# Multiply before the first half of the down weights: a reordering on VectorE in an expert loop

## The chip, the cores and the metric

The kernel runs on one core of one Trainium2 chip. The metric is device time in microseconds (us) for one launch that computes both request groups through both layers. Each engine of the core (TensorE or PE, VectorE or DVE, ScalarE or ACT, GpSimd or POOL, SyncE or SP) has its own instruction stream, runs it in order, and meets the others only through semaphores.

## The reference, cut to what matters

Two layers of an encoder work on 2 x 256 tokens of width 1024. In each layer an attention part is followed by a mixture of experts, and the change is in the latter:

```
for e in range(16):
    a   = silu(t @ w_gate[e]) * (t @ w_up[e])        # 512 wide
    out = out + gate[:, e:e+1] * (a @ w_down[e])     # 1024 wide
```

`gate` is zero but for two experts of each token. The inputs and weights are float32.

## The kernel before, in words

**Tiles.** After the router, VectorE works out a plan: the chosen (token, expert) pairs are sorted by expert into tiles of 128 rows with one expert each. In the run shown here there are 16 tiles in each layer, 14 in a loop over pairs of tiles and two behind it (`last=True`). A tile is even (`par` 0) or odd (`par` 1); each parity has its own ring slots for weights and its own half of the row buffers.

**Two-part arithmetic.** A product of float32 matrices is made of three products of a faster format. ScalarE copies a weight half (128x2048) into a high part (`high`, line 1293) and VectorE subtracts that from the original to get the low part (`low`, line 1865). TensorE then runs low x high, high x low and high x high into one bank (lines 947 to 949 for gate and up, 962 to 964 for down). A tile has six such halves, or parts: up 0 and 1, gate 0 and 1, down 0 and 1; each is 12 matmuls. The high parts go round four buffers, so part number `at + i` waits until part `at + i - 4` has been used (`part_used`).

**Order on TensorE in tile n:** transposes of the gathered rows of tile n+1 (line 927, waits for the gather); up 0 and up 1 of n; gate 0 of n+1; transposes of the activated rows of n (line 935, waits for `a_ready`); gate 1 of n+1; down 0 and down 1 of n (wait for `aT_lo_ready` and the low parts). In what follows a tile's start is the start of its line 927.

**Order on ScalarE in tile n:** high part of the rows of n+1 (line 1300); SiLU of the gate result of n (line 1314); `high` of gate 1 of n+1 (at+3), of down 0 (at+4) and of down 1 (at+5); `aT_hi`, the high part of the transposed activation (line 1321); `high` of up 0, up 1 and gate 0 of the tiles that follow (at+6, at+7, at+8); the two copies of the result to `y_row` (line 1330).

**Order on VectorE in tile n:** low part of the rows of n+1 (line 1874); `low` at+3; `low` at+4; the multiplication of SiLU and up (line 1891), which waits until up 1 is done (`part_used`) and for `silu_ready`, and raises `a_ready`; `low` at+5; `aT_lo` (line 1894), which waits for `aT_hi`; `low` at+6, at+7, at+8. The `low` instructions read two tiles of SBUF; lines 1874, 1891 and 1894 read one bank of PSUM and one tile of SBUF.

**Order on GpSimd in tile n:** copy the row indices for tile n+2 (`row_now`, line 1975), drain, gather its rows from HBM (line 1957); wait for the result of tile n (`y_ready`), copy its indices (line 1975), drain, scatter its rows to HBM (line 1962); wait until they have landed. As this is one stream, the gather of tile n+3 is issued only after the scatter of tile n has landed. The gather issued while TensorE is in tile n+1 is the one whose rows are transposed at the start of tile n+2.

**SyncE** loads 2 MB of weights for each of gate, up and down of each tile, each as soon as the part that frees its slot has been used (line 631).

Of the kernel before, what the change touches and what calls it, by code (L numbers as in the profile page):

```python
# [303 lines left out]
def build_trunk(nc, t_in, y_prompt, y_sample):  # L304
# [7 lines left out]
    with ctx:  # L312
# [1049 lines left out]
        def _(dve):  # L1362
# [25 lines left out]
            at = PAR["b_ada"]  # L1388
# [10 lines left out]
            at = PAR["neg_lam"]  # L1399
# [116 lines left out]
            with dve.Fori(0, DEPTH) as layer:  # L1516
# [344 lines left out]
                def low(k, par, h, buf, at):  # L1861

                    dve.wait_ge(part_hi_ready, at + 1)
                    cols = slice(h * 2048, (h + 1) * 2048)
                    v.tensor_tensor(w_low[EXPERT_SLOTS[par][k]][:, cols], ring[EXPERT_SLOTS[par][k]][:, cols],  # L1865
                                    part_hi[buf].bitcast(F32), ALU.subtract)\
                        .then_inc(part_lo_ready, 1)

                def rows_low(n, par):

                    dve.wait_ge(xg_hi_ready, n + 1)
                    for half in range(2):
                        at = (slice(None), par, slice(4 * half, 4 * half + 4), slice(None))
                        ins = v.tensor_tensor(xg_lo[at].rearrange("p c n -> p (c n)"), bank[4 + half][:, :],
                                              xg_hi[at].rearrange("p c n -> p (c n)").bitcast(F32), ALU.subtract)
                    ins.then_inc(xg_lo_ready, 1)

                def expert(p, par, last=False):
                    n = (before + p) * 2 + par
                    ends_here = last and par == 1  # L1880
                    first = 2 + 6 * par
                    at = (before + p) * 12 + first
                    buf = [(first + i) % 4 for i in range(9)]
                    if not ends_here:
                        rows_low(n + 1, 1 - par)
                        low(0, 1 - par, 1, buf[3], at + 3)
                    d = 2 if ends_here else 4
                    low(2, par, 0, buf[d], at + d)
                    dve.wait_ge(part_used, PARTS_BEFORE + at + 2)
                    dve.wait_ge(silu_ready, n + 2)  # L1890
                    v.tensor_tensor(act_rows, bank[1][:, :], silu[:, par, :], ALU.mult).then_inc(a_ready, 1)
                    low(2, par, 1, buf[d + 1], at + d + 1)
                    dve.wait_ge(aT_hi_ready, n + 1)
                    v.tensor_tensor(aT_lo.rearrange("p f n -> p (f n)"), bank[6][:, :],
                                    aT_hi.rearrange("p f n -> p (f n)").bitcast(F32), ALU.subtract)\
                        .then_inc(aT_lo_ready, 1)
                    if not ends_here:
                        for h in range(2):
                            low(1, 1 - par, h, buf[6 + h], at + 6 + h)
                    if not last:  # L1900
                        low(0, par, 0, buf[8], at + 8)
# [7 lines left out]
                with dve.Fori(0, rest) as p:  # L1909
                    for par in range(2):  # L1910
                        expert(p, par)
                for par in range(2):
                    expert(rest, par, last=True)
# [111 lines left out]
```

## Time and profile before

| | us |
|---|---|
| Median of 3 runs (1803.8 to 1806.64) | 1805.65 |
| The profiled execution's own time | 1801.19 |
| Its span, first to last instruction | 1799.3 |
| PE busy (matmul) | 1523.4 (85%) |
| DVE busy | 1052.2 (58%) |
| ACT busy | 886.8 (49%) |
| POOL busy | 136.5 (8%) |

The two expert loops take about 540 to 884 us and 1411 to 1755 us of the span. Busy time is a share over the whole span; what is late in a stretch is read from the waits and from the order of time. A row of the time line gives start and duration in us, engine, line, operation, tiles, shapes and count, and in brackets the idle time of the engine before it and what ended it. Rows that follow each other closely may be merged (x2), and their first number is then the start of the first. The duration of a DMA row on POOL is that of issuing it, not of the transfer.

### The profile page before, as it was taken

To read this page: it belongs to the slowest core of one execution; us is meant where nothing else is said; L and a number is where in the kernel's file an instruction comes from. 1 tells how busy PE (TensorE), PEld (TensorE's weight loads), DVE (VectorE), ACT (ScalarE), POOL (GpSimd) and SP (SyncE) were. 2 spreads that over 40 slices of the span, in tenths; PEclk is the share of its full clock that TensorE was granted. 3 is DMA by queue.
4 is the path that set the end of the run, shared out by engine and by line. 5 is a ranking of instruction groups with operands and counts; after the bars stand their busy time and mean duration, and the time that the engine had idled before them with its cause. 6 is when DMAs were issued, how large, how long until landed. Compare 5 with 4: busy or idle time off the path is not lost.

```text
span 1799.3 us, 19037 instructions
## 1 busy us (share of the span) xinstructions
PE 1523.4 (85%) x6494; PEld 1081.9 (60%) x6494; DVE 1052.2 (58%) x1339; ACT 886.8 (49%) x1146; POOL 136.5 (8%) x141
## 2 busy tenths in 40 slices
PE   3799987999957999999469989799997489999984
PEld 1477545666725777777327765466664477777762
DVE  2645469222466788778253825942244688778755
ACT  2532348111236777786244224731133477777743
POOL 2000000000001121211000000000000112121200
PEclk9899997999977999999789989799998699999997
DMA  8622570111237999998392147202113789999923
GB/s 244 226 94 94 188 234 1 47 47 52 89 141 275 346 346 339 334 336 298 131 326 94 47 141 257 71 22 72 47 50 137 254 307 348 322 336 338 324 100 143
DMA packets 164692, 341.82 MB, mean 190 GB/s; under 512 B 26214, under 2 KB 28912, under 8 KB 164496
## 3 DMA queue, kind: packets, MB, share of 16 engines
q1 hardware_dynamic: 150752, 314.58, 50.0%
q0 software_dynamic: 10800, 23.09, 3.4%
q10 hardware_dynamic: 3072, 3.28, 0.7%
q8 instruction: 38, 0.62, 0.1%
q14 instruction: 30, 0.25, 0.0%
HBM read 333.58 MB, written 24.12 MB: 199 GB/s over the span
## 4 chain that ended last, share of the span: by engine, by line
PE 58%; DVE 11%; ACT 9%; issue 9%; DMA 8%; SPq 3%; ACTq 1%; POOLq 1%; DVEq 0%
PE bank L684 9%; PE bank L685 8%; PE bank L686 8%; PE bank L879 6%; DMA y_by_choice<-zone,row_now 3%; DMA zone<-rows_by_token,row_now 3%; PE bank L962 3%; PE bank L964 3%; PE bank L963 3%; PE bank L715 2%; SPq L582 2%; PE bank L832 2%; PE bank L947 2%; PE bank L949 2%; PE bank L948 2%
## 5 line engine op out<-in xcount | busy, mean ns | idle before, releaser
L684 PE MATMUL bank<-x_hi,w_lo 128*128 128x512 f32 x608 | 257.3, 423 | 20.0 <-DVE x_lo L1451 8.4
L686 PE MATMUL bank<-x_hi,w_hi 128*128 128x512 f32 x608 | 238.2, 392 | 0.0
L685 PE MATMUL bank<-x_lo,w_hi 128*128 128x512 f32 x608 | 238.2, 392 | 0.0
L1865 DVE TENSOR_TENSOR w_lo<-ring,zone_r 128x2048 fp32r<-128x2048 f32 x92 | 210.4, 2290 | 27.6 <-ACT zone_r L1293 27.6
L1293 ACT CAST x_lo<-ring 128x2048 fp32r<-128x2048 f32 x96 | 183.6, 1914 | 66.5 <-PE bank L949 30.7
L1293 ACT CAST zone_r<-ring 128x2048 fp32r<-128x2048 f32 x96 | 181.6, 1910 | 20.4 <-PE bank L964 13.9
L947 PE MATMUL bank<-w_lo,zone_r 128*128 128x512 f32 x384 | 160.2, 417 | 5.8 <-issue 5.8
L684 PEld LDWEIGHTS bank<-x_hi,w_lo 128*128 128x128 f32 x608 | 114.9, 189 | 62.2 <-issue 30.0
L1428 DVE TENSOR_TENSOR w_lo<-ring,w_hi 128x1024 fp32r<-128x1024 f32 x84 | 102.0, 1221 | 85.1 <-ACT w_hi L1088 84.6
L685 PEld LDWEIGHTS bank<-x_lo,w_hi 128*128 128x128 f32 x608 | 115.2, 190 | 31.3 <-issue 9.6
L686 PEld LDWEIGHTS bank<-x_hi,w_hi 128*128 128x128 f32 x608 | 115.0, 189 | 24.6
L1251 ACT ACTIVATE zone<-bank 128x512 f32<-128x512 f32 x32 | 19.1, 597 | 216.7 <-PE bank L686 216.7
L1865 DVE TENSOR_TENSOR w_lo<-ring,x_lo 128x2048 fp32r<-128x2048 f32 x36 | 82.3, 2292 | 61.4 <-ACT x_lo L1293 61.4
L879 PE MATMUL bank<-zone,ring 128*128 128x512 f32 x256 | 115.8, 595 | 0.9
L948 PE MATMUL bank<-x_lo,zone_r 128*128 128x512 f32 x272 | 111.0, 408 | 0.0
L949 PE MATMUL bank<-x_lo,zone_r 128*128 128x512 f32 x272 | 110.9, 408 | 0.0
L1088 ACT CAST w_hi<-ring 128x1024 fp32r<-128x1024 f32 x84 | 87.1, 1044 | 22.9 <-DMA ring<-in_w_in 6.1
L949 PE MATMUL bank<-zone_r 128*128 128x512 f32 x240 | 94.9, 395 | 0.0
L948 PE MATMUL bank<-zone_r 128*128 128x512 f32 x240 | 94.4, 393 | 0.0
L947 PEld LDWEIGHTS bank<-w_lo,zone_r 128*128 128x128 f32 x384 | 75.3, 196 | 21.9 <-issue 6.6
L715 PE MATMUL bank<-ring,cs 128*32 128x512 f32 x384 | 53.8, 684 | 36.1 <-DMA ring<-in_w_ada 35.6
L1954 POOL DMA_DIRECT2D rows_by_token<-zone x8 | 4.4, 548 | 999.2 <-ACT zone L1280 998.4
(255 smaller groups left out, 2743.6 us busy)
## 6 DMA issues: line engine op xcount, KB each, us to landing
ring<-in_w_gate SPq DMA_DIRECT2D x32, 2048.0 KB, 13.7
ring<-in_w_up SPq DMA_DIRECT2D x32, 2048.0 KB, 14.7
ring<-in_w_down SPq DMA_DIRECT2D x32, 2048.0 KB, 9.2
ring<-in_w_ada SPq DMA_DIRECT2D x24, 2048.0 KB, 8.8
ring<-in_w_in SPq DMA_DIRECT2D x14, 2048.0 KB, 7.9
ring<-in_w_out SPq DMA_DIRECT2D x4, 2048.0 KB, 7.7
zone<-y_by_choice SPq DMA_DIRECT2D x8, 1024.0 KB, 8.1
ring<-in_w_in SPq DMA_DIRECT2D x16, 256.0 KB, 7.1
```

The lines of the kernel that those rows point to most:

```text
L684: mm(out, lo, x_first, start=start, stop=False)
L685: mm(out, hi, x_second, start=False, stop=False)
L686: return mm(out, hi, x_first, start=False, stop=stop)
L715: ins = mm(ps[32 * j:32 * (j + 1), :], cs[:, k, :], w[:, k, :], start=(k < 4), stop=(k >= KC - 4))
L879: ins = mm(ps[:, :], w[:, k, j * P:(j + 1) * P], oT[:, k, :], start=(k == 0), stop=(k == 3))
L947: mm(out, xg_hi[:, par, c, :], wv[:, c, :], start=(c == 0), stop=False)
L948: mm(out, xg_lo[:, par, c, :], hi[:, k, :], start=False, stop=False)
L949: ins = mm(out, xg_hi[:, par, c, :], hi[:, k, :], start=False, stop=(c == KC - 1))
L1088: nc.scalar.copy(w_hi[:, n % W_BUFS, :, :], group_view(ring[SLOT[b]], b, c)).then_inc(S["w_hi_ready"], 1)
L1293: nc.scalar.copy(part_hi[buf], ring[EXPERT_SLOTS[par][k]][:, h * 2048:(h + 1) * 2048])\
L1428: v.tensor_tensor(group_view(w_lo[SLOT[b]], b, c), group_view(ring[SLOT[b]], b, c), w_hi[:, n % W_BUFS, :, :].bitcast(F32), ALU.subtract). ...
L1865: v.tensor_tensor(w_low[EXPERT_SLOTS[par][k]][:, cols], ring[EXPERT_SLOTS[par][k]][:, cols], part_hi[buf].bitcast(F32), ALU.subtract)\
```

## The change

One line of VectorE's part of the expert loop moves down, behind the multiplication. Its waits go with it (they are inside `low`).

```diff
                         low(0, 1 - par, 1, buf[3], at + 3)
                     d = 2 if ends_here else 4
-                    low(2, par, 0, buf[d], at + d)
                     dve.wait_ge(part_used, PARTS_BEFORE + at + 2)
                     dve.wait_ge(silu_ready, n + 2)
                     v.tensor_tensor(act_rows, bank[1][:, :], silu[:, par, :], ALU.mult).then_inc(a_ready, 1)
+                    low(2, par, 0, buf[d], at + d)
                     low(2, par, 1, buf[d + 1], at + d + 1)
```

The helper that it calls:

```
                def low(k, par, h, buf, at):
                    dve.wait_ge(part_hi_ready, at + 1)
                    cols = slice(h * 2048, (h + 1) * 2048)
                    v.tensor_tensor(w_low[EXPERT_SLOTS[par][k]][:, cols], ring[EXPERT_SLOTS[par][k]][:, cols],
                                    part_hi[buf].bitcast(F32), ALU.subtract)\
                        .then_inc(part_lo_ready, 1)
```

`part_lo_ready` counts in the same order as before: the order of the `low` instructions among themselves does not change. No instruction is added or removed.

## Rows read from the trace of the kernel before

**Rows 1.** The page, its fourth part: the chain that ended last, by line.

```profile
PE bank L684 9%; PE bank L685 8%; PE bank L686 8%; PE bank L879 6%; DMA y_by_choice<-zone,row_now 3%; DMA zone<-rows_by_token,row_now 3%; PE bank L962 3%; PE bank L964 3%; PE bank L963 3%; PE bank L715 2%; SPq L582 2%; PE bank L832 2%; PE bank L947 2%; PE bank L949 2%; PE bank L948 2%
```

**Rows 2.** PE's waits: us, times, longest; L935 twice: first, then second layer's loop.

```profile
PE bank L935 <- DVE root L1891: 14.3, 15, 2.4
...
PE bank L935 <- DVE root L1891: 16.3, 16, 2.5
...
PE bank L927 <- DMA zone<-rows_by_token,row_now: 7.5, 8, 1.4
```

**Rows 3.** Busy time by stretch, two pairs of tiles; the last three: clock, DMA share, GB/s.

```profile
1511.44:1551.53 40.09, 36.87 (x169) 29.20 (x169) 32.12 (x21) 31.31 (x27) 8.27 (x8) 1.00 0.97 348
...
1591.64:1633.12 41.48, 38.24 (x169) 30.51 (x169) 32.08 (x21) 31.13 (x26) 8.09 (x8) 0.96 0.92 330
```

**Rows 4.** Time line of PE in the pair 1511.44 to 1551.53.

```profile
1511.44 1.09 PE L927 MATMUL bank<-const,zone 128*128 128x128 f32 x8 [1.10 <-DMA zone<-rows_by_token,row_now]
...
1522.72 0.66 PE L935 MATMUL bank<-const,root 128*128 128x128 f32 x4 [1.87 <-DVE root L1891]
...
1526.02 0.39 PE L962 MATMUL bank<-w_lo,zone_r 128*128 128x512 f32 x1
...
1531.72 1.09 PE L927 MATMUL bank<-const,zone 128*128 128x128 f32 x8
...
1541.40 0.66 PE L935 MATMUL bank<-const,root 128*128 128x128 f32 x4 [0.21 <-DVE root L1891]
...
1551.53 1.09 PE L927 MATMUL bank<-const,zone 128*128 128x128 f32 x8 [1.09 <-DMA zone<-rows_by_token,row_now]
```

**Rows 5.** Time line of DVE in the same pair, around the multiplications.

```profile
1517.57 2.29 DVE L1865 TENSOR_TENSOR w_lo<-ring,x_lo 128x2048 fp32r<-128x2048 f32 x1 [2.41 <-ACT x_lo L1293]
1519.78 2.29 DVE L1865 TENSOR_TENSOR w_lo<-ring,zone_r 128x2048 fp32r<-128x2048 f32 x1
1521.98 0.68 DVE L1891 TENSOR_TENSOR root<-bank,tmp 128x512 f32<-128x512 f32 x1
1522.58 2.28 DVE L1865 TENSOR_TENSOR w_lo<-ring,zone_r 128x2048 fp32r<-128x2048 f32 x1
1524.78 0.69 DVE L1894 TENSOR_TENSOR zone_r<-bank,zone_r 128x512 fp32r<-128x512 f32 x1
...
1538.46 2.28 DVE L1865 TENSOR_TENSOR x_hi<-ring,x_lo 128x2048 fp32r<-128x2048 f32 x1
1540.66 0.68 DVE L1891 TENSOR_TENSOR root<-bank,tmp 128x512 f32<-128x512 f32 x1
1541.26 2.28 DVE L1865 TENSOR_TENSOR x_hi<-ring,x_lo 128x2048 fp32r<-128x2048 f32 x1
1543.46 0.68 DVE L1894 TENSOR_TENSOR zone_r<-bank,zone_r 128x512 fp32r<-128x512 f32 x1
1544.51 4.59 DVE L1865 TENSOR_TENSOR w_lo<-ring,zone_r 128x2048 fp32r<-128x2048 f32 x2 [0.37 <-ACT zone_r L1293]
```

**Rows 6.** Time line of POOL in the same pair.

```profile
1512.82 1.02 POOL L1962 DMA_INDIRECT y_by_choice<-zone,row_now  x1 [0.94 <-issue]
1521.39 0.71 POOL L1975 COPY row_now<-row_i 128x1 int32 x1 [7.55 <-DMA y_by_choice<-zone,row_now]
1523.05 2.71 POOL L1957 DMA_INDIRECT zone<-rows_by_token,row_now  x1 [0.94 <-issue]
...
1542.35 1.23 POOL L1975 COPY row_now<-row_i 128x1 int32 x1 [6.98 <-DMA y_by_choice<-zone,row_now]
1544.49 1.02 POOL L1957 DMA_INDIRECT zone<-rows_by_token,row_now  x1 [0.91 <-issue]
```

**Rows 7.** Line L1957 in the second layer: durations (min/median/max) and its transfers.

```profile
L1957 POOL DMA_INDIRECT zone<-rows_by_token,row_now x14: 1012/1028/2725, 1423.2 to 1707.8; - x14
...
DMA to landing us min/median/max: 6.4/7.4/8.8
```

**Rows 8.** Time line of ACT in the odd tile of that pair.

```profile
1542.09 0.59 ACT L1321 CAST zone_r<-bank 128x512 fp32r<-128x512 f32 x1 [1.73 <-PE bank L935]
1542.57 1.91 ACT L1293 CAST zone_r<-ring 128x2048 fp32r<-128x2048 f32 x1
```

## The prediction

> **What bounds the kernel now.** I read the chain that ended last, then PE's waits in the loops, then one pair of tiles instruction by instruction. The chain [rows 1] holds two entries that are no engine's work: the scatter of results and the gather of rows, 3% each, some 54 us each of 1799. So in the loops there is a path through GpSimd and the DMA besides the one through PE. PE's waits [rows 2] say the same: it waits for the multiplication (L1891) 14.3 + 16.3 = 30.6 us in the two loops, about once in each tile, and for the gather in every second tile. The first wait is what the edit aims at; the second may take its place.
>
> The pair 1511.44 to 1551.53 is a plain one: granted clock 1.00 (the 2.4 GHz level), 40.09 us, DMA engines 97% busy at 348 GB/s [rows 3]. Its even tile takes 1531.72 - 1511.44 = 20.28 us and its odd tile 19.81 us [rows 4]. In the even tile PE waits 1.87 us for the multiplication, in the odd one 0.21 us. The next even tile starts only when its gather has landed (1.09 us of idle time, 1.10 in front of this one). The odd tile starts with none shown, but 1531.72 is also 5.96 us after its own gather was issued (1523.05 + 2.71 = 1525.76 [rows 6]), and the other gather took 6.02 us from the end of its issue (1544.49 + 1.02 = 1545.51) to PE's start at 1551.53. So both starts hang on gathers, the odd one just so.
>
> Now how GpSimd and VectorE meet. The gather in the odd tile is issued in 1.02 us, the one in the even tile in 2.71 us; 1.03 is the median of the 14 and 2.73 the maximum [rows 7]. The long one started at 1523.05 inside a `low` (1522.58 to 1524.86 [rows 5]) and ended 0.90 us after it. The small index copies do the same: that of 1542.35 ended at 1543.58, 0.04 after the `low` that ran until 1543.54; that of 1521.39 ended at 1522.10, 0.03 after the `low` that ran until 1522.07, though the multiplication had by then begun. I read this as: a GpSimd instruction that begins while a `low` (two SBUF inputs) runs waits for its end, and the multiplication and `aT_lo` (one PSUM input) let it through. The gather at 1544.49 was spared narrowly: the next `low` began at 1544.51, 0.02 us behind it, and only because VectorE had been idle for 0.37 us for ScalarE.
>
> The **Trainium skill** (SBUF — State Buffer, section "Who interferes with whom") says that a DVE instruction with two SBUF inputs contends with a GpSimd instruction that reads SBUF, and the later one blocks fully until the first has finished; by the rows above the trace agrees for the copies. The same section infers that a tensor_tensor does not stall descriptor generation, as that needs only the write side. By that inference the gathers would never be held by a `low` and the time would be that of the rival "no change" below; the 2.71 us speak against it, so I don't follow it.
>
> **The change, part by part.** The multiplication waits for up 1 and SiLU, both done before `low` at+3 ends in either tile, so it moves ahead by one `low`, 2.20 us (1521.98 - 1519.78).
>
> Even tile. The multiplication runs 1519.78 to 1520.46; PE had nothing else to do from 1522.72 - 1.87 = 1520.85 on, so that wait is gone. What is late next is `aT_lo`: the three instructions `low` at+4, multiplication, `low` at+5 take the same time in any order, so it still ends at 1525.47. Down 0 starts then instead of at 1526.02 [rows 4]: the gain is about 0.5 us out of 1.87. The odd tile could start 0.5 us earlier, but its gather has to be there.
>
> Odd tile. In the same way 0.2 to 0.4 us of PE are saved (its wait, 0.21 as shown; up to 0.38 when the overlap of matmuls is counted). ScalarE's `aT_hi` (1542.09) and the `high` of at+6 behind it (1542.57 to 1544.48 [rows 8]) come earlier by as much: that `high` ends at 1544.1 to 1544.3. And here the cover goes: `low` at+6 no longer waits for ScalarE. It starts right behind `aT_lo`, at 1544.1 to 1544.3 instead of 1544.51. The gather does not move: its index copy was held until the end of `low` at+5 (1543.54, unchanged), and the drain of 0.91 puts it at 1544.49. Now it is 0.2 to 0.4 us behind the start of a `low` instead of 0.02 in front. It waits for the end of `low` at+6 (1544.13 + 2.29 = 1546.42) and ends 0.90 later, at 1547.32 instead of 1545.51: 1.81 us late. With 6.02 us to landing the next even tile starts at 1553.34: the odd tile takes 21.62 instead of 19.81 us.
>
> Back in the even tile, the scatter of the odd tile before it was sent in time while the tile started 1.8 + 0.4 us later, so it lands 2.2 us earlier against the tile's start: 1521.39 becomes about tile + 7.7 instead of tile + 9.95. The index copy is then held by `low` at+3 (until tile + 8.4) and slips through at the multiplication. The gather starts at tile + 9.3, is held by `low` at+4 (until tile + 11.2) and ends at about tile + 12.1 instead of tile + 14.32; it lands at tile + 18.1 and PE finishes the tile at tile + 19.6, which now sets the odd start. Even tile 19.6 instead of 20.28.
>
> The new pair: 19.6 + 21.6 = 41.2 us, 1.1 us more. Of the 16 tiles of a layer, counted from 0, the odd ones 1 to 13 each issue a gather on which the start of the next even tile (2 to 14) hangs: seven in each layer, 14 x 1.1 = 15.5 us. Off go about 0.9 us in each layer for the last two tiles, which have no gather behind them (-1.8), and about 1.5 us for the pairs in which the clock fell to 0.96 and PE took 41.48 us [rows 3], part of which is now hidden behind the gather. Sum: +12 us.
>
> **Unknown sizes, from both sides.** (1) DMA from gather issue to landing: from the shortest (6.4 - 1.02 = 5.4 us) to the longest (8.8 - 2.72 = 6.1) [rows 7]. The delayed gather meets a little less weight traffic. At 5.4 the odd tile is 21.0 us, the pair 40.6, the sum +4. Below that the scatter lands in the even tile's `low` at+4 as now and the even tile goes back to 20.3, so a held gather can hardly gain. I take 6.0, which both of this pair's gathers show. (2) Whether GpSimd gets in between two `low` instructions with no gap. No row of before shows a GpSimd instruction begun in the first of two such. If it does, the wait is as above. If VectorE keeps what they share, the gather waits for at+7 too, 2.2 us more: odd tile 23.8, pair 43.4, 14 x 3.3 - 1.8 = +45 us. I take the first: at the border between a `low` and a multiplication GpSimd was let in 0.03 us after the `low` ended. (3) VectorE itself being held by GpSimd: the `low` behind the gather at 1544.49 began and lasted as the others, so nothing.
>
> **Rivals.**
> A, the forecast: the odd gather is caught by `low` at+6 and released behind it. +12 us, range +3 to +20.
> B: caught and held over two `low` instructions, +45 us. For it: the two are adjacent, with the second ready; against it: point (2).
> C, no change: the odd gather gets through (a lead of 0.2 to 0.4 us is shorter than the 0.47 at which 1523.05 was caught, and the skill's inference of above would also let it through), or its transfer catches up. Then both starts still hang on gathers that do not move: even tile 20.28, odd 19.81, and only the last tiles gain. -2 to +3 us.
> D, the other side, faster: PE's order decides and the gathers follow. It is decided by the landing: if gathers take less than about 5.5 us, or index copies fall into a multiplication's gap and not into a `low`, PE gains its 0.5 + 0.4 us in each of the 16 pairs (8 in each layer): at most 14 us, as `aT_lo` is next. For it: tiles with PE at once behind the gather's landing exist, the even start waits only 1.1 us. Against it: the gather chain is in the chain of the end [rows 1] and nothing of the edit shortens it. A naive reader would take the whole 30.6 us; `aT_lo` excludes that. -5 to -14 us.
>
> **Numbers.** A 0.54, B 0.18, C 0.13, D 0.15. The sum was made against the profiled execution: 1801.19 + 12 = 1813.2 (its span 1799.3, with 1.9 around it). The runs' median lies 4.5 above that execution, and I add the 12 to the median: 1805.65 + 12 = 1817.6, rounded to 1817.5. A alone: 1809 to 1826. The range reaches from just under the median, cutting most of D, up to B's 1805.65 + 46: 1801 to 1852. A measurement of this kernel can tell about 0.2% (3.6 us) from no change: faster is D, 0.15; the same is C and A's edge, 0.14; slower 0.71.
>
> **What would show it.** PE's wait for L1891 falls from 30.6 us to near nothing, and a wait for `aT_lo` (L1894) appears before L962, 1.0 to 1.5 us in even tiles. POOL's L1957 in odd tiles lasts about 2.8 us instead of 1.02 (B: about 5), and ends 0.9 behind the end of a `low`. PE's wait in front of even tiles for the gather grows from 1.1 to about 3.3 us; pairs take about 41.2 us. I am wrong if L1957 in odd tiles stays at 1.02 us, or if it is longer and the even tiles still start 19.8 us after the odd ones; and my reading of the stall falls if instructions held on POOL don't end with a `low`.

## The result, and the profile after

| | before | changed |
|---|---|---|
| Median of 4 runs | 1804.72 us | 1823.44 us |
| Lowest to highest | 1798.8 to 1806.64 | 1814.78 to 1828.55 |
| Profiled execution | 1801.19 us | 1814.78 us |

The ratio on record is 1.0089, 95% interval 1.0059 to 1.0118: 16 us slower, 11 to 21 by the interval (the two medians alone lie 18.7 apart). 1817.5 had been forecast (+12), slower with a chance of 0.71.

The chain that ended last (the page, its fourth part) now has more of the gathers and scatters, 7% and 6% where there were 3% each [rows 1]:

```profile
PE bank L684 8%; PE bank L686 8%; PE bank L685 8%; DMA zone<-rows_by_token,row_now 7%; DMA y_by_choice<-zone,row_now 6%; PE bank L879 6%; DVE w_lo L1865 2%; PE bank L962 2%; PE bank L715 2%; SPq L582 2%; PE bank L832 2%; PE bank L964 2%; PE bank L963 2%; PE bank L947 2%; PE bank L949 2%
```

PE's waits in the two loops (total us, times, longest), first layer, then second. They answer to [rows 2]. The multiplication is now line 1890.

```profile
PE bank L927 <- DMA zone<-rows_by_token,row_now: 21.1, 7, 4.0
...
PE bank L962 <- DVE w_lo L1865: 9.2, 7, 1.4
...
PE bank L935 <- DVE root L1890: 0.9, 1, 0.9
...
PE bank L927 <- DMA zone<-rows_by_token,row_now: 21.2, 7, 3.3
...
PE bank L962 <- DVE w_lo L1865: 5.0, 4, 1.4
```

The wait for the multiplication is gone (30.6 us before, one of 0.9 left). In its place stand 7 waits of some 3 us in each layer for the gather, and, in most even tiles, one of 1.4 in front of down 0. The last are labelled with `low` (L1865); VectorE's order below shows that the `aT_lo` behind it (line 1894, 1573.39 to 1574.07) is what ends just before down 0 starts at 1574.27.

One pair of tiles, PE, then DVE, then POOL (start, duration, engine, line), to be laid beside [rows 4 to 6]:

```profile
1560.23 1.09 PE L927 MATMUL bank<-const,zone 128*128 128x128 f32 x8 [3.16 <-DMA zone<-rows_by_token,row_now]
...
1574.27 0.50 PE L962 MATMUL bank<-w_lo,zone_r 128*128 128x512 f32 x1 [1.39 <-DVE w_lo L1865]
1579.88 1.03 PE L927 MATMUL bank<-const,zone 128*128 128x128 f32 x8
...
1601.55 1.09 PE L927 MATMUL bank<-const,zone 128*128 128x128 f32 x8 [3.15 <-DMA zone<-rows_by_token,row_now]
```

```profile
1568.99 4.48 DVE L1865 TENSOR_TENSOR w_lo<-ring,zone_r 128x2048 fp32r<-128x2048 f32 x2
1573.39 0.68 DVE L1894 TENSOR_TENSOR zone_r<-bank,zone_r 128x512 fp32r<-128x512 f32 x1
...
1586.66 0.68 DVE L1890 TENSOR_TENSOR root<-bank,tmp 128x512 f32<-128x512 f32 x1
1587.27 4.48 DVE L1865 TENSOR_TENSOR x_hi<-ring,x_lo 128x2048 fp32r<-128x2048 f32 x2
1591.67 0.68 DVE L1894 TENSOR_TENSOR zone_r<-bank,zone_r 128x512 fp32r<-128x512 f32 x1
1592.27 4.51 DVE L1865 TENSOR_TENSOR w_lo<-ring,zone_r 128x2048 fp32r<-128x2048 f32 x2
```

```profile
1561.06 1.03 POOL L1962 DMA_INDIRECT y_by_choice<-zone,row_now  x1 [2.45 <-issue]
1569.25 2.07 POOL L1975 COPY row_now<-row_i 128x1 int32 x1 [7.17 <-DMA y_by_choice<-zone,row_now]
1572.24 2.12 POOL L1957 DMA_INDIRECT zone<-rows_by_token,row_now  x1 [0.93 <-issue]
...
1590.76 1.03 POOL L1975 COPY row_now<-row_i 128x1 int32 x1 [7.03 <-DMA y_by_choice<-zone,row_now]
1592.70 2.74 POOL L1957 DMA_INDIRECT zone<-rows_by_token,row_now  x1 [0.91 <-issue]
```

In the odd tile `low` at+6 begins at 1592.27 and the gather at 1592.70, 0.43 us behind it. The gather takes 2.74 us instead of 1.02 and ends at 1595.44, 0.9 us behind the first of the two `low` instructions (1592.27 + 2.29 = 1594.56), not behind the second. All 14 gathers of odd tiles took 2.74 to 2.76 us. The odd tile takes 21.67 us, the even one 19.65: 41.3 us for the pair.

Where the whole time went, by stretch (length, then busy time of PE, PEld, DVE, ACT, POOL; granted clock, DMA share, GB/s). Each kernel: tiles 0 to 14 of layer 1, its last pair up to the last scatter, what lies between the loops, and the two loop stretches of layer 2. First the kernel before:

```profile
561.25:844.09 282.84, 260.41 (x1178) 206.72 (x1176) 226.00 (x141) 218.10 (x182) 53.93 (x52) 0.99 0.91 327
844.09:882.91 38.82, 31.97 (x136) 25.08 (x136) 19.93 (x14) 18.23 (x18) 3.53 (x6) 0.96 0.20 72
882.91:1431.53 548.62, 455.18 (x1890) 301.12 (x1891) 264.22 (x488) 197.57 (x362) 6.57 (x9) 0.90 0.38 131
1431.53:1714.83 283.30, 260.49 (x1177) 206.88 (x1175) 225.87 (x141) 217.90 (x182) 53.00 (x52) 0.99 0.92 328
1714.83:1753.69 38.86, 31.99 (x136) 25.09 (x136) 19.96 (x14) 18.26 (x18) 3.55 (x6) 0.95 0.18 63
```

and the changed one:

```profile
561.26:850.31 289.05, 258.52 (x1177) 206.00 (x1175) 224.01 (x141) 217.58 (x182) 63.99 (x53) 0.99 0.90 321
850.31:892.26 41.95, 33.15 (x136) 25.97 (x136) 19.37 (x13) 18.21 (x17) 3.36 (x5) 0.92 0.14 56
892.26:1434.88 542.62, 451.02 (x1891) 300.62 (x1892) 264.31 (x488) 197.74 (x362) 6.74 (x9) 0.91 0.39 132
1434.88:1724.72 289.84, 263.08 (x1177) 209.50 (x1176) 224.36 (x141) 217.73 (x182) 64.78 (x53) 0.98 0.90 322
1724.72:1767.22 42.50, 33.70 (x136) 26.42 (x136) 19.53 (x13) 18.32 (x17) 3.38 (x5) 0.88 0.12 49
```

The loops up to tile 14 are 6.2 + 6.5 = 12.8 us longer, the last pairs 3.1 + 3.6 = 6.8 us. Together 19.5 us, of which the stretch between the loops, where nothing was changed, gives 6.0 us back in this execution (548.62 to 542.62). So the loops lose more than the 13.6 us between the two profiled executions, and the 16 us of the ratio lie between the two figures.

The last pair's loss, which I had not forecast, has a place. In the last tile PE goes from its transposes straight to down 0 (PE, layer 1; before, then changed):

```profile
869.19 0.66 PE L935 MATMUL bank<-const,root 128*128 128x128 f32 x4 [0.87 <-DVE root L1891]
872.13 0.49 PE L962 MATMUL bank<-x_hi,zone_r 128*128 128x512 f32 x1 [2.28 <-DVE x_hi L1865]
```

```profile
875.16 0.66 PE L935 MATMUL bank<-const,root 128*128 128x128 f32 x4 [0.87 <-DVE root L1890]
880.30 0.79 PE L962 MATMUL bank<-x_hi,zone_r 128*128 128x512 f32 x1 [4.49 <-DVE x_hi L1865]
```

From the transposes to down 0 it is 5.14 us instead of 2.94. There the `low` of down 0 used to run while VectorE waited for up 1. Behind the multiplication it is in the open, and no part of gate 1 lies in between to hide it. The first matmul of layer 1 also shows the lower clock level (0.79 us against 0.49; in layer 2 it is 0.79 against 0.69). PE's busy time in the last pairs grows by 1.2 and 1.7 us at the same 136 matmuls, which is the rest of the 3.1 and 3.6 us.

### The profile page after: what moved, and what is told of

Same layout as the page of the kernel before. It is cut to its first block, busy times and chain, and to the rows that moved or that the text cites. A ratio compares the mean times of both kernels' runs of the same rounds, so it can differ in the third digit from the quotient of the medians.

```text
span 1812.8 us, 19037 instructions
## 1 busy us (share of the span) xinstructions
PE 1524.7 (84%) x6494; PEld 1087.5 (60%) x6494; DVE 1047.8 (58%) x1339; ACT 886.4 (49%) x1146; POOL 158.0 (9%) x141
## 4 chain that ended last, share of the span: by engine, by line
PE 55%; DMA 15%; DVE 11%; issue 8%; ACT 7%; SPq 3%; POOLq 1%; ACTq 1%; DVEq 0%
PE bank L684 8%; PE bank L686 8%; PE bank L685 8%; DMA zone<-rows_by_token,row_now 7%; DMA y_by_choice<-zone,row_now 6%; PE bank L879 6%; DVE w_lo L1865 2%; PE bank L962 2%; PE bank L715 2%; SPq L582 2%; PE bank L832 2%; PE bank L964 2%; PE bank L963 2%; PE bank L947 2%; PE bank L949 2%
## 5 line engine op out<-in xcount | busy, mean ns | idle before, releaser
L684 PE MATMUL bank<-x_hi,w_lo 128*128 128x512 f32 x608 | 257.4, 423 | 19.8 <-DVE x_lo L1451 8.4
L1865 DVE TENSOR_TENSOR w_lo<-ring,zone_r 128x2048 fp32r<-128x2048 f32 x92 | 208.0, 2287 | 26.8 <-ACT zone_r L1293 26.8
L1865 DVE TENSOR_TENSOR w_lo<-ring,x_lo 128x2048 fp32r<-128x2048 f32 x36 | 82.4, 2292 | 65.6 <-ACT x_lo L1293 65.6
L949 PE MATMUL bank<-zone_r 128*128 128x512 f32 x240 | 97.2, 405 | 0.0
L948 PE MATMUL bank<-zone_r 128*128 128x512 f32 x240 | 96.6, 402 | 0.0
L927 PE MATMUL bank<-const,zone 128*128 128x128 f32 x256 | 38.0, 297 | 61.4 <-DMA zone<-rows_by_token,row_now 42.3
```

What stands on the lines that cost most here:

```text
L684: mm(out, lo, x_first, start=start, stop=False)
L927: ins = nc.tensor.transpose(bank[4 + c // 4][:, (c % 4) * P:(c % 4 + 1) * P], xg[:, par, c * P:(c + 1) * P], K("ident"))
L948: mm(out, xg_lo[:, par, c, :], hi[:, k, :], start=False, stop=False)
L949: ins = mm(out, xg_hi[:, par, c, :], hi[:, k, :], start=False, stop=(c == KC - 1))
```

## The experiments

All are on one core, timed in five rounds beside runs of the kernel before on the same chip. The tile times are medians of the distances between the starts of PE's row transposes (L927), both layers; even ones without tile 0. They and the last column come from one profiled execution of each kernel, the ratio from all its runs.

| kernel | ratio to before (95%) | even tile | odd tile | tiles 0 to 14, per layer |
|---|---|---|---|---|
| before | 1 | 20.38 | 19.81 | 282.8, 283.3 |
| changed | 1.0089 (1.0059 to 1.0118) | 19.65 | 21.59 | 289.1, 289.8 |
| even tiles only | 0.9943 (0.9922 to 0.9964) | 20.29 | 19.81 | 280.5, 281.0 |
| odd tiles only | 1.0090 (1.0062 to 1.0118) | 20.23 | 21.57 | 292.0, 292.7 |
| not the last tile | 1.0045 (1.0024 to 1.0066) | 19.95 | 21.56 | 291.9, 289.2 |
| before + two memsets on GpSimd | 1.0084 (1.0050 to 1.0117) | 20.46 | 21.86 | 294.9, 294.9 |
| changed, `low` behind GpSimd's queue | 1.0102 (1.0075 to 1.0128) | 19.95 | 21.82 | 293.0, 292.8 |
| changed, `low` behind the gather | 0.9932 (0.9910 to 0.9954) | 20.12 | 19.81 | 279.4, 279.0 |
| gather first, old order | 1.0004 (0.9988 to 1.0020) | 22.26 | 19.16 | 285.5, 285.7 |
| gather first, new order | 0.9931 (0.9906 to 0.9955) | 20.47 | 18.91 | 276.2, 275.2 |
| gather first, new but last tile | 0.9878 (0.9853 to 0.9904) | 20.49 | 18.95 | 276.3, 275.1 |
| the same, no drain | 0.9857 (0.9833 to 0.9881) | 21.11 | 18.36 | 275.0, 275.4 |
| changed, no drain | 1.0071 (1.0046 to 1.0097) | 19.65 | 21.52 | 289.3, 289.1 |
| before, no drain | 0.9981 (0.9962 to 1.0000) | 20.49 | 19.76 | 285.5, 282.9 |

**Half of the edit at a time.** `mult_first` chooses the order in three kernels:

```diff
+                    mult_first = par == 0 and not last   # or: par == 1 and not last; or: not ends_here
+                    if not mult_first:
+                        low(2, par, 0, buf[d], at + d)
                     dve.wait_ge(part_used, PARTS_BEFORE + at + 2)
                     dve.wait_ge(silu_ready, n + 2)
                     v.tensor_tensor(act_rows, bank[1][:, :], silu[:, par, :], ALU.mult).then_inc(a_ready, 1)
-                    low(2, par, 0, buf[d], at + d)
+                    if mult_first:
+                        low(2, par, 0, buf[d], at + d)
```

Even tiles only:

> The reordering in even tiles of the loop alone; odd tiles and the last pair keep the old order. My theory (the loss is the odd tile's gather, caught by the low of part at+6): L1957 in odd tiles stays at 1.02 us, odd tiles take 19.8 us, even tiles 20.0 to 20.3 because their gather still hangs on the end of the low at+5; pairs 39.8 to 40.1 us, time -3 to +2 us against the kernel before. Rival (any moved low delays something in its own tile, DVE bunches up): about a third to a half of the measured loss, +5 to +8 us.

Odd tiles only:

> The reordering in odd tiles of the loop alone. My theory: L1957 in odd tiles 2.75 us and their time 21.6 us as in the changed kernel; even tiles in the old order keep their wait for the multiplication, 20.0 to 20.3 us; pairs 41.6 to 41.9 us instead of 40.1, so 14 x 1.5 to 1.8 = +21 to +25 us, more than the whole change cost though half of it is undone. Rival (each tile's reordering costs its share): +5 to +8 us.

All but the last tile:

> The change, but the very last tile of each layer (where no gate part lies between up 1 and down 0) keeps the old order. Theory: the trace of the changed kernel has the last tile's down 0 start 5.14 us after its transposes instead of 2.94, since its low now lies behind a multiplication that waits for up 1; so 2.2 us come back in each layer, up to 3.5 if the clock drop that follows goes too: 4.4 to 7 us faster than the changed kernel, about +10 to +13 us against before. Rival (the 3 us more behind the last gather are the clock's alone): same as the changed kernel, +16.

Even tiles alone make the kernel faster, by 0.57%; odd tiles alone cost as much as both. The loss sits in the odd tile, 21.6 against 19.8 us, and is no sum of equal shares, so the rival of equal shares falls. Two sizes missed. The even-only kernel gained 10 us where -3 to +2 was expected; its tiles 0 to 14 gained 2.4 and 2.3 us, 4.7 together, which is also more than the 3. The kernel before has three even tiles of 21.66, 21.66 and 22.25 us at a granted clock of 0.92, each with a wait for the multiplication of 1.87 to 2.46 us; the even-only kernel, without these waits, has no even tile over 20.82 us. Together they are some 4.7 us above the usual 20.3, which is the size of the gain, though not shown to be all of it. Its profile gains the other 6 us outside the two loops, in code that is the same in both. A part of that goes with the clock: over the 23 runs of before of this comparison the time fell by 11.2 us for each 0.01 of mean granted clock (correlation -0.76), and the even-only kernel's 12 runs had 0.936 against 0.929. At equal clock 5 us are left, by an estimate from these figures. Why the clock was granted more often outside the loops I did not settle. The odd-only kernel lost 16 us and not 21 to 25, though in its profile tiles 0 to 14 are 9.2 and 9.4 us longer, 18.6 together; that difference stays open.

Without the last tile the changed kernel is at +8 us instead of +16, an 8 us difference from two comparisons with intervals of some 4 to 5 us each. In both layers' profiles the down part starts 2.94 us behind the transposes again. So the last tile costs its 2.2 us in each layer; what is above 4.4 is within the two intervals, and nothing shows a cause for it.

**A nudge on GpSimd alone.** VectorE is as before; the index copy ahead of a gather is followed by two memsets:

```diff
                     nc.gpsimd.tensor_copy(now, row_i[:, which, bass.ds(tile, 1)]).then_inc(index_now, 1)
+                    if which == 0:
+                        for _ in range(2):
+                            nc.gpsimd.memset(pool_scratch[:, _, :], 0.0)
                     nc.gpsimd.drain()
```

> The kernel before, VectorE untouched; on GpSimd two memsets of 128x32 (about 0.1 us each) stand between the index copy and the drain ahead of every gather in the loop. My theory: the odd tile's gather starts 0.1 to 0.2 us later, behind the start of the low of at+6 instead of 0.02 us in front, is held, and takes about 2.6 us instead of 1.02: odd tiles about 21.6 us, pairs 41.6 to 41.9, +20 to +25 us. Rival (nothing is held; a delay costs itself): at most 14 x 0.2 x 2 = +3 to +6 us, L1957 in odd tiles 1.02 us.

The gather and the `low` of an odd tile in its trace (POOL, then DVE):

```profile
1555.80 0.77 POOL L1976 COPY row_now<-row_i 128x1 int32 x1 [7.28 <-DMA y_by_choice<-zone,row_now]
...
1557.59 3.11 POOL L1958 DMA_INDIRECT zone<-rows_by_token,row_now  x1 [0.89 <-issue]
```

```profile
1557.50 4.59 DVE L1866 TENSOR_TENSOR w_lo<-ring,zone_r 128x2048 fp32r<-128x2048 f32 x2 [0.37 <-ACT zone_r L1294]
```

A gather that starts 0.09 us behind a `low` takes 3.11 us; one that starts 0.02 us in front of it takes 1.02 [rows 6]. So it is with all 14: in the kernel before the gather starts 0.01 to 0.03 us in front of the `low`, here 0.08 to 0.09 behind it, and each takes 3.11 to 3.13 us. The ratio is that of the changed kernel within the intervals, +15 us, without any edit on VectorE. A delay that cost itself would have been 3 to 6 us. The +20 to +25 expected were missed on the low side by the ratio; in its profile tiles 0 to 14 are 12.0 and 11.6 us longer, 23.6 together. So the expectation held in the loops of the profiled execution and not in the ratio, and why is open.

**Holding the low back.** The changed kernel, with a wait ahead of `low` at+6 in odd tiles. First with a semaphore that GpSimd's queue raises behind the gather (`nc.gpsimd.sem_inc(gather_sent, 1)`):

> The changed kernel, and in odd tiles of the loop VectorE waits before the low of at+6 until GpSimd has issued its gather. It makes VectorE later by about 1.4 us in each odd tile and takes nothing away. My theory: the odd tile's gather takes 1.02 us again and ends 13.85 us behind the tile's start, odd tiles take 19.8 us, even ones 20.0 to 20.3, pairs 40.1; the time is 11 to 16 us under the changed kernel's, within -3 to +5 us of the kernel before (the last tile still costs 2 us in each layer). Rival (the loss is VectorE's own lateness or the moved low): no better than the changed kernel, +16 us or more, since VectorE is later still.

That failed as an experiment (a kernel near the time of before was expected), and shows something. The queue ran ahead of the engine: the `low` began at 675.16, the gather at 675.24.

```profile
675.24 3.12 POOL L1960 DMA_INDIRECT zone<-rows_by_token,row_now  x1 [0.91 <-issue]
```

```profile
675.16 4.49 DVE L1866 TENSOR_TENSOR w_lo<-ring,zone_r 128x2048 fp32r<-128x2048 f32 x2 [0.27 <-POOLq L1989]
```

So it was one more kernel with the gather held (+18 us). The second form raises the semaphore by an instruction of the engine:

```diff
                         gather(par, index_of(0, tile + 2, par))
+                    if par == 1:
+                        nc.gpsimd.memset(pool_scratch[:, 0, :], 0.0).then_inc(gather_sent, 1)
...
+                    if par == 1 and not last:
+                        dve.wait_ge(gather_sent, before + p + 1)
                     if not ends_here:
                         for h in range(2):
                             low(1, 1 - par, h, buf[6 + h], at + 6 + h)
```

> The changed kernel; in odd tiles of the loop GpSimd runs a memset of 128x32 behind the gather, and VectorE's low of at+6 waits for that memset. (In the run before of this kind the wait was released when GpSimd's queue passed it, 0.08 us before the gather began, so the low was still first.) My theory: the odd tile's gather takes 1.02 to 1.1 us and ends 13.85 us behind the tile's start; VectorE is 1.5 us later; odd tiles 19.8 us, even ones 20.0 to 20.3, pairs about 40.1; 12 to 18 us under the changed kernel, within -5 to +5 us of before. Rival (VectorE's order is at fault, GpSimd isn't): the changed kernel's time or more, +16 us or more.

```profile
677.81 1.03 POOL L1961 DMA_INDIRECT zone<-rows_by_token,row_now  x1 [0.91 <-issue]
678.83 0.15 POOL L1991 MEMSET pool_scratch<- 128x32 f32 x1
```

```profile
679.11 4.49 DVE L1867 TENSOR_TENSOR w_lo<-ring,zone_r 128x2048 fp32r<-128x2048 f32 x2 [1.64 <-POOL pool_scratch L1991]
```

VectorE waits 1.64 us more in each odd tile, and the kernel is 12 us faster than before: 1.6% under the changed one, whose ratio was 1.0089. All 14 gathers of odd tiles are back at 1.02 to 1.04 us and the odd tile at 19.81 us. This is the sharpest test: making the edited engine later undoes the loss. Both intervals exclude VectorE's own order as the cause. It came out better than the -5 to +5 expected: its tiles 0 to 14 are 3.5 and 4.3 us shorter than before, with one even tile at a clock of 0.92 where the kernel before has four at 0.91 to 0.92, and the last tiles' loss is still in it. The rest goes with a higher clock, as with the even-only kernel (mean of its runs 0.937, of before 0.928).

**Taking the scatter out of the gathers' chain.** GpSimd issues the gather before it waits for the last scatter to land. The wait moves into a helper, `stored_up_to`, and the first two tiles stand in front of the loop (cut to what matters):

```diff
                         gather(par, index_of(0, tile + 2, par))
+                    if not first:
+                        stored_up_to(p - 1 + par, 1 - par)
                     pool.wait_ge(y_ready, n + 2)
                     nc.gpsimd.sem_inc(passed, 1)
                     scatter(par, index_of(1, tile, par))
-                    pool.wait_ge(y_sent[par], (before + p) * 16 + 16)
-                    nc.gpsimd.sem_inc(y_stored[par], 16)
```

With the old order of VectorE, with the new, and with the new but in the last tile:

> VectorE in the old order; on GpSimd the gather of tile n+2 is issued as soon as its rows' buffer is free, and only then does GpSimd wait for the scatter before (the first two tiles of a layer are peeled off the loop for it). That takes the scatter's landing out of the chain of the gathers. Theory: PE's waits for gathers vanish, even tiles 20.0 us (bound by the wait for the multiplication), odd ones 18.7, pairs 38.7 to 39.3 (the DMA engines, 97% busy in pairs of 40.1, then are at their end), 14 x 0.8 to 1.4 = -11 to -20 us. Rival (the DMA engines' 97% are the bound already, the gathers are only where it shows): -3 to +2 us.

> The same on GpSimd with the changed order on VectorE, last tile included. Theory: with no gather behind the scatter the edit's own gain shows, 0.5 + 0.4 us in each pair down to where aT_lo or the DMA engines bind: pairs 37.9 (by PE) to 38.9 (by DMA), against e6 -14 x 0.3 to 0.9, + 4.4 for the two last tiles: -8 to +1 us against e6, and -15 to -25 against before, where the same edit alone cost 16. Rival (the edit is bad by its own order on VectorE): about 16 us slower than e6.

> As e7, but the very last tile of each layer keeps the old order of VectorE. Theory: 4.4 us faster than e7 (2.2 in each layer), which would make it the fastest version, -19 to -30 us against before. Rival (the last tile's 2.2 us are hidden by the scatter and the copy behind it): the same as e7 within 1 us.

With the old order nothing is won; with the new order the same edit that cost 16 us is worth 16 (1808.0 to 1792.21), and 24 without the last tile. The sizes missed: -11 to -20 us had been expected of the first kernel and 0 came; the second was to be at most 8 us faster than the first and is 16. Against before it is at -12 us and not -15 to -25; the third, at -22, is within its -19 to -30. Why the first kernel won nothing is in its trace (POOL, PE, then two stretches with the clock):

```profile
645.42 1.02 POOL L1962 DMA_INDIRECT y_by_choice<-zone,row_now  x1 [0.94 <-issue]
646.45 0.20 POOL L1975 COPY row_now<-row_i 128x1 int32 x1
654.44 1.13 POOL L1957 DMA_INDIRECT zone<-rows_by_token,row_now  x1 [7.79 <-DMA y_by_choice<-zone,row_now]
```

```profile
655.32 0.66 PE L935 MATMUL bank<-const,root 128*128 128x128 f32 x4 [2.91 <-DVE root L1891]
```

```profile
643.00:655.00 12.00, 9.41 (x44) 7.50 (x44) 7.53 (x6) 10.67 (x10) 1.97 (x4) 1.00 0.97 357
655.00:665.00 10.00, 9.68 (x38) 7.88 (x39) 7.65 (x5) 6.03 (x4) 0.57 (x1) 0.83 0.89 333
```

The gather still left only when the scatter had landed, 7.79 us behind its index copy, though no semaphore asks for that: the drain is what stands between them. But the copy is out of the way, so gathers come sooner and even tiles from tile 4 on wait at most 0.6 us for them. The wait for the multiplication then grows in one piece, to 2.91 us here, and behind it the granted clock falls from 1.00 to 0.83. Ten even tiles of the two loops have such a wait of 2.45 to 3.19 us. Eight of them have a mean clock of 0.92 to 0.93 and take 22.2 to 22.9 us; the two that stay at 1.00 take 20.7 and 20.8. With the new order that wait is at most 0.9 us, and the clock is 1.00 in both loops (0.98 and 0.97 with the old one).

**A semaphore in place of the drain.**

```diff
-                    nc.gpsimd.drain()
+                    pool.wait_ge(index_now, n * 2 + which + 1)
...
```

> As e8 (gather issued ahead of the wait for the scatter's landing, changed order but for the last tile), and GpSimd waits for its index copy by a semaphore instead of a drain. Theory from e6 to e8: the drain doesn't pass while an indirect DMA of GpSimd is in flight, so the gather still went out 7.8 us behind the scatter; without it the gather goes out 1 to 3 us behind the tile's start, no start of a tile waits for one, and pairs go from 39.4 to 38.0 to 38.9 us: 5 to 14 us faster than e8, -27 to -36 us against before. Rival (the 7.8 us are something else that the gather waits for, or the DMA engines bind at 93%): the same as e8.

> The changed kernel with GpSimd's order as before, but a semaphore wait in place of the drain behind each index copy. Theory: the odd tile's gather goes out 0.1 to 0.2 us behind the end of the low of at+5, while aT_lo runs and before the low of at+6, so it takes 1.02 us and ends at about tile + 13.0: odd tiles 19.0 to 19.2 us, even ones 19.6, pairs 38.7 instead of 41.3: -12 to -20 us against before, 30 us under the changed kernel. Rival (the held gather is not the loss): 14 x 2 x 0.8 us of drains at most, and still above the kernel before's time less 10.

> The kernel before (old order of VectorE) with the same semaphore wait in place of the drains. Theory: even tiles PE-bound at 20.0 us, odd ones 19.0, pairs 39.0 where the clock holds; but as in e6 PE then waits 2.6 to 3.1 us in one piece for the multiplication and the clock falls to its lower level in some pairs, so -10 to 0 us against before; the edit's own worth is then e12 minus e11: 5 to 15 us gained by the very order that costs 16 with the drains.

With the gather first and no drain the kernel is the fastest, 0.9857 of before, 1782.07 us. The even tile's gather leaves 2.1 us behind its scatter (POOL), and no start in the loops waits for one:

```profile
639.28 1.02 POOL L1966 DMA_INDIRECT y_by_choice<-zone,row_now  x1 [0.88 <-POOL row_now L1979]
640.30 0.20 POOL L1979 COPY row_now<-row_i 128x1 int32 x1
641.36 1.03 POOL L1961 DMA_INDIRECT zone<-rows_by_token,row_now  x1 [0.85 <-POOL row_now L1979]
```

That shows that it was the drain that held it. But it is only some 2 to 4 us better than with the drain (medians 1784.03 and 1782.07, the intervals overlap), less than the 5 to 14 expected: in even tiles PE waits 1.0 us for the multiplication and 1.7 us in front of down 0 again. The pairs stay at 39.5 us, at a DMA share of 0.97; which of the two limits binds is not shown:

```profile
637.57:677.03 39.46, 36.75 (x169) 29.24 (x168) 30.71 (x21) 30.78 (x27) 7.14 (x8) 1.00 0.97 351
```

The other two missed their main point. I had taken the 0.9 us between copy and gather for the drain's, so that the gather would slip in front of the `low` without it. The semaphore takes 0.85 us as well: the gather is still held (2.8 us), odd tiles stay at 21.52 us, and the ratio (1.0071) is the changed kernel's within the intervals, where -12 to -20 us had been expected. With the old order it gives at best a trifle (-3 us, interval -7 to 0), so the edit does not gain the 5 to 15 us between these two kernels that I had expected: the pair of them repeats its cost, about 0.9%, where a gather is held.

## Why the prediction was right

**The place and the price of the loss were right.** The multiplication 2.2 us earlier, about 0.5 us of gain in the even tile before `aT_lo` ends it, the odd gather behind the start of `low` at+6 and held to its end + 0.9: 2.74 us for 1.02, odd tile 21.59 for the 21.62 forecast, even 19.65 for 19.6 (medians). The nudge and the kernel with the `low` behind the gather show that this is the cause, from either side.

**The open question between A and B** (is the gather held over two adjacent `low` instructions) was answered for A: it ends 0.9 us behind the first. Index copies do likewise: the one at 1569.25 ended at 1571.32, between two `low` instructions that began at 1568.99 and ran on to 1573.47.

**The step that failed: the -1.8 us for the last two tiles, taken off because no gather is behind them.** They cost 3.1 and 3.6 us, +6.8 for -1.8. I treated the last tile as an odd tile of the loop, but its `low` had been free there and no gate part hides it. That is 2.2 us in each layer, with more matmul time at a lower clock on top. The loop term itself was near: 14 x 1.1 less 1.5 is 14, and 12.8 was measured. So the profile puts the loops and the last pairs at 19.5 us where the sum has 12. That the total came out nearer is in part luck: in the profiled execution the stretch between the loops, which the edit does not touch, gave 6.0 us back.

**A second step was off without effect.** The scatter of the odd tile did not go out in time against the even tile: it was issued 0.83 us behind its start (1561.06, 2.45 us behind the copy), where the sum had it at about -0.8 (1512.82 - 1511.44 less 2.2). The drain in front of it lasted until the gather had landed, which I did not foresee. The scatter landed at tile + 9.0 and not + 7.7, the copy was held in the next `low`, and the gather ended at tile + 14.1 (1574.36) and not + 12.1. Still PE shows no wait at the start of the odd tile, 5.5 us later (1579.88). So the even tile's 19.6 was right, and my way to it in part luck.

**Rival D** (faster) is excluded with this chain in place, but its idea was right: free of the chain, the edit is worth 16 to 24 us, more than the 14 I gave as its most, since it also avoids the stretches of lower clock. The 24 are with the old order kept in the last tile.

## What to carry to other kernels

Before an instruction of VectorE with two SBUF inputs is moved, look at which of GpSimd's instructions it then overtakes: here 0.02 us in front or 0.09 us behind the start of a `low` decided over 2.1 us in every second tile (a gather of 1.02 or of 3.11 us), and the engine that lost time was not the one edited. A wait removed by reordering shows its worth only when the chain that ends last with it is loosened; try the edit again after each such step, by parity and by the last tile apart, since the same line cost 0.9% and gained 0.9%. A stagger that holds one engine back by 1.6 us can be the cheaper repair.

## What the runs showed of the hardware

**The drain of GpSimd** waited for its indirect DMA in flight: 7.79 us in the kernel with the gather first, and 2.45 us in the changed one (0.94 where nothing is in flight). With a semaphore wait the next DMA left 0.85 to 0.89 us behind the copy in either case; in the changed kernel without drains one scatter left at 1598.76, 0.57 us before the start of the tile that was waiting for the gather in flight (1599.33).

**The shared port, narrower than its rule.** The **Trainium skill** (SBUF — State Buffer, section "Who interferes with whom") calls the port pair that VectorE and GpSimd share an exclusive lock, and has a VectorE instruction with two SBUF inputs contend with a GpSimd instruction that reads SBUF. The traces agree for GpSimd behind VectorE, also when the next `low` is adjacent: it is let in between the two. The other way round they show less: a `low` that began 0.02 us behind the gather's start was not held for the gather's 1.02 us and lasted 2.30 us (2.29 otherwise). The section's inference that a tensor_tensor leaves descriptor generation alone is not borne out by these gathers (2.7 to 3.1 us against 1.02). They also read their row indices from SBUF (`row_now`); no run separates that read from the making of descriptors. The section on the chip says that the engines meet only through semaphores; here GpSimd and VectorE meet at this port as well.

**The clock after a wait.** One wait of 2.91 us of PE was followed by a stretch of 0.83; with the new order on VectorE tiles stayed at 1.00. It did not follow every such wait. In the changed kernel the even tile behind the wait of 3.16 us for the gather, and the odd tile after it, are at 1.00:

```profile
1560.23:1579.88 19.65, 18.25 (x84) 14.74 (x85) 14.04 (x10) 14.56 (x11) 5.22 (x3) 1.00 0.88 326
1579.88:1601.55 21.67, 18.48 (x85) 14.51 (x83) 17.74 (x11) 16.62 (x15) 5.35 (x5) 1.00 0.96 338
```

Of its 12 even tiles from tile 2 on that begin behind such a wait (2.4 to 4.0 us), five have 0.91 to 0.93 and seven 1.00. What decides between them no run here shows.
